# A triangular inverse in a RWKV stage: its 128x128 transposes become 64x64 products with an identity

## The reference, cut to what matters

```
def step(S, inp):
    wt, kkt, kat, kt, vt, rt = inp
    S = (S * wt[..., None, :]
         - jnp.einsum('...vk,...k->...v', S, kkt)[..., :, None] * kat[..., None, :]
         + vt[..., :, None] * kt[..., None, :])
    return S, jnp.einsum('...vk,...k->...v', S, rt)
```

## Time and profile before

| | |
|---|---|
| median of 3 runs | 1917.11 us (1916.86 to 1919.38) |
| profiled execution, its span (the time that its profile gives) | 1921.7 us |
| PE busy | 1734.6 us, 90% of the span |
| granted TensorE clock, mean | 0.948 of full speed |
| RWKV stage, both directions with what lies between | about 606 to 864 us |

### The profile page before, as it was taken

One profiled execution on the slowest core, in us unless ns is written; L12 is line 12 of the kernel. 1 busy time (PEld: TensorE's weight loads), 2 busy tenths in 40 slices (PEclk: granted clock), 3 DMA queues, 4 the chain that ended last, 5 costly groups with the idle time before them and its releaser, 6 DMA issues.

```text
span 1921.7 us, 32920 instructions
## 1 busy us (share of the span) xinstructions
PE 1734.6 (90%) x14129; PEld 1449.6 (75%) x14129; DVE 736.9 (38%) x1219; ACT 639.3 (33%) x1208; POOL 550.2 (29%) x498
## 2 busy tenths in 40 slices
PE   7997899799876983989999787999999999999998
PEld 5886778688655762768997686888888888888886
DVE  3105888233175547554232425120332133113307
ACT  4214887323255432433243424221211112111122
POOL 4213753221044315315234010222222222222221
PEclk9998999899878995998999997999999999999999
DMA  5110000121000000002312010111111111111112
GB/s 183 50 59 1 1 1 1 31 69 34 17 1 6 4 3 0 5 3 98 128 59 85 17 47 20 49 46 49 50 50 45 55 49 41 48 56 49 45 44 93
DMA packets 61200, 81.27 MB, mean 42 GB/s; under 512 B 4610, under 2 KB 49824, under 8 KB 61056
## 3 DMA queue, kind: packets, MB, share of 16 engines
q1 hardware_dynamic: 60112, 76.60, 12.9%
q0 software_dynamic: 944, 2.58, 0.6%
HBM read 74.96 MB, written 4.19 MB: 41 GB/s over the span
## 4 chain that ended last, share of the span: by engine, by line
PE 79%; DVE 11%; ACT 5%; issue 2%; DMA 1%; POOL 1%; SPq 0%; DVEq 0%; ACTq 0%
PE PS L1511 13%; PE PS L1512 13%; PE PS L1514 13%; PE PS L1764 7%; PE PS L2064 4%; PE PS L2062 4%; PE PS L2063 4%; PE PS L1524 4%; PE PS L1525 3%; PE PS L1526 3%; PE PS L1622 3%; PE PS L1656 2%; PE PS L1828 2%; PE PS L1648 1%; DVE E__70 L1083 1%
## 5 line engine op out<-in xcount | busy, mean ns | idle before, releaser
L421 POOL TENSOR_TENSOR WL<-RAW,WH 128x512 fp32r<-128x512 f32 x226 | 308.6, 1375 | 945.5 <-ACT WH L581 945.4
L1511 PE MATMUL PS<-HH,WH 128*128 128x512 f32 x1072 | 420.7, 392 | 10.9 <-POOL WL L421 8.0
L1512 PE MATMUL PS<-HL,WH 128*128 128x512 f32 x1072 | 419.6, 391 | 0.0
L581 ACT ACTIVATE WH<-RAW 128x512 fp32r<-128x512 f32 x226 | 140.2, 631 | 642.9 <-PE PS L1514 310.2
L1514 PE MATMUL PS<-HH,WL 128*128 128x512 f32 x1072 | 331.5, 391 | 0.0
L1511 PEld LDWEIGHTS PS<-HH,WH 128*128 128x128 f32 x1072 | 202.7, 189 | 53.9 <-issue 8.3
L1514 PEld LDWEIGHTS PS<-HH,WL 128*128 128x128 f32 x1072 | 202.5, 189 | 42.4
L1512 PEld LDWEIGHTS PS<-HL,WH 128*128 128x128 f32 x1072 | 202.9, 189 | 41.9
L1461 DVE TENSOR_TENSOR FU<-PS,ACTB 128x512 f32<-128x512 f32 x44 | 27.3, 684 | 469.1 <-PE PS L1514 469.1
L2062 PE MATMUL PS<-WH,AH 128*128 128x512 f32 x352 | 136.9, 389 | 0.0
L2063 PE MATMUL PS<-WL,AH 128*128 128x512 f32 x352 | 136.9, 389 | 0.0
(11 more groups left out here) (296 smaller groups left out, 2817.0 us busy)
## 6 DMA issues: line engine op xcount, KB each, us to landing
RAW<-in_ffn_w_gu SPq DMA_DIRECT2D x88, 256.0 KB, 2.8
RAW<-in_w_in SPq DMA_DIRECT2D x48, 256.0 KB, 2.8
RAW<-in_ffn_w_down SPq DMA_DIRECT2D x44, 256.0 KB, 2.6
XT<-in_x SPq DMA_DIRECT2D x8, 512.0 KB, 5.1
RAW<-in_w_out SPq DMA_DIRECT2D x16, 256.0 KB, 2.7
X<-in_x SPq DMA_DIRECT2D x8, 512.0 KB, 8.3
RAW<-in_x_wkv SPq DMA_DIRECT2D x16, 256.0 KB, 2.7
out_x<-FO SPq DMA_DIRECT2D x8, 512.0 KB, 2.6
```

The lines of the kernel that those rows point to most:

```text
L421: pool.tensor_tensor(w_low, RAW[:, p % NRAW], w_high.bitcast(F32), ALU.subtract).then_inc(w_lo, 1)
L581: act.activation(split_at(p)[0], RAW[:, p % NRAW], ACT.Copy).then_inc(w_hi, 1)
L1511: pe.matmul(where(ct, i), wh[:, k, c], ah(kt)[:, t0:t0 + n], start=first and starts(ct, i), stop=False, skip_group_check=True)
L1512: pe.matmul(where(ct, i), wh[:, k, c], al(kt)[:, t0:t0 + n], start=False, stop=False, skip_group_check=True)
```

## The change

Each turn of Q is made by eight 64x64 products, Q's block as the stationary operand and a 64x64 identity as the moving one, in the order of `blocks()`, in place of two 128x128 transposes. The output of block (ct, hp, c) now goes to bank c at column 64 ct. So the two readers take it from there, and the copies stay as they are.

```diff
 def inverse_t(j):
-    for ct in range(2):
-        mm = pe.transpose(PS[:, (j.slot.a, j.slot.b)[ct], 256:384], j.slot.Q[:, 2 * ct:2 * ct + 2, :].rearrange("p h k -> p (h k)"), ID)
+    for ct, hp, c, rh, rc in blocks():
+        mm = mm1(PS[rh, (j.slot.a, j.slot.b)[c], 256 + 64 * ct:320 + 64 * ct], j.slot.Q[rc, 2 * ct + hp, :], I64[rc])
     return mm
...
 def inverse(j, l):
...
-        mm = mm1(PS[rc, (sl.a, sl.b)[hp], 64 * ct:64 * ct + 64], sl.XQ[rh, ct, 3, c, :], sl.XQ[rh, c, 2, ct, :])
+        mm = mm1(PS[rc, (sl.a, sl.b)[hp], 64 * ct:64 * ct + 64], sl.XQ[rh, c, 3, ct, :], sl.XQ[rh, c, 2, ct, :])
...
 def wu(j):
...
-        mm = mm1(PS[rc, (sl.a, sl.b)[hp], P * ct:P * ct + P], sl.XQ[rh, ct, 3, c, :], sl.XQ[rh, c, 0:2, ct, :])
+        mm = mm1(PS[rc, (sl.a, sl.b)[hp], P * ct:P * ct + P], sl.XQ[rh, c, 3, ct, :], sl.XQ[rh, c, 0:2, ct, :])
```

## The result

The changed kernel takes 1937.63 us (median of 4 runs, 1933.82 to 1943.67), the kernel before in the same comparison 1918.24 us (1916.86 to 1922.29). The ratio is 1.0097, with an interval of 1.0071 to 1.0123: about 19 us slower, where 12 us faster was forecast.

A forecast was written before the change was run, and what follows sets the result against it. PE, 90% busy, with a nearly full queue and a DVE tail, bounds the steady period. Savings of 3.7 + 0.3 + 0.7 + 0.4 + 0.55 + 0.1 = 5.75 us a direction, 11.5 for both, give 1917.1 - 11.5 = 1905.6 us; range 1899 to 1913.

The forecast's parts named there:

- the walk: Step-by-step timing of the stage through engine queues and waits, with a turn at 0.235 us: 5.75 us saved a direction.
- Rival 1: At each turn: only two quarters overlap, so the products cost 0.47 us; 1915 us in all; chance 0.12.
- Rival 2: In the steady periods: more PE idle time lowers the clock to 1.2 GHz, slower, from 1921.6 us; chance 0.05.
- Rival 3: In each fill: products instead of transposes raise the clock earlier, 5 us more gain, 1900.6 us; chance 0.12.
- one steady period: From one job's turn to the same turn of the next: 11.50 us becomes 10.76, five such a direction, 3.7 us.
- the chain from 611.12 to 630.93: First periods of the stage, a chain of single steps: said to hold six turns, with gains of 0.3 and 0.7 us.
- The fill's terms: Gains while the stage fills, a direction: 0.3 us first period, 0.7 for the next three turns, 0.4 third period.

The follow-up runs named there:

- experiment 1: Kernel before with 28 or 14 empty instructions ahead of each turn, or 224 ahead of each feed-forward step: ratios 0.9997, 1.0002, 1.0010.

## Why the prediction was wrong

**What it got right.** A turn on quarters holds PE for 0.24 us, as taken from the nearest row, and the cost ahead of it is gone. The floor of 25 ns from start to start, which the prediction cites from the Trainium skill (TensorE: Matmul & The Clock Gate, "Wait — 56ns, not 53.3ns?"), is contradicted once more: 16 records in 0.24 us. Where no issue wait falls the walk holds roughly: with one turn changed, steady periods of 11.35 us where it gave 0.18 less than 11.49, and a first period (from the first key transposes to the second) of 8.55 us in the changed kernel, where the kernel before took 8.83 in another execution (its program ran again in experiment 1) and the walk gave 0.3 less. In the second period it gave too much: 0.7, where 9.07 to 9.16 became 8.80.

**The rivals.** Rival 1 is out: the turn takes 0.24 us. Rival 2, the falling clock, came in small: two stretches at 0.5 in the second direction's steady part, 6.8 us together. It isn't the cause, since the first direction had 1.00 in all its steady periods and was late all the same, by 6.6 us. The prediction had argued against it from 701 to 705 us, where PE was busy 1.86 of 4 us at 1.00; in the same trace the clock fell to 0.5 at 705.7 and stayed there to 712.5. Rival 3 isn't seen: the first period has a second stretch at 0.5 in two executions of the kernel before (10.65 us) and none in two others (8.83), so this goes by the execution.

**The step that failed** is the sum of "one steady period": the walk had PE, DVE, ACT and POOL in it, but not the supply of PE's program. It came to 10.76 us with 938 instructions (so many the trace has from one steady period to the next), 3.7 blocks of 256, so 2.9 us a block. Nothing in it asked whether a block can be had in 2.9 us. The pace while PE was short of instructions was 3.69 us a block (numbers 7617 to 10689, 634.49 to 678.80, in the changed kernel). That gives 938 / 256 x 3.69 = 13.5 us; 13.5 and 13.1 were measured. The first of these holds the stretch from which the pace was read and is no test of it; the second, and the other kernels in the table above, are. The kernel before, with 770, needs 11.1 us by the same pace and ran at 11.49: it was 0.4 us from this bound, and its cheap turns of four instructions in 0.57 us were what kept it off. The prediction came near it once. It noted 15 ns for a record, 7.5 ns for an instruction, as a proof that 16 small products are cheap. That is the rate within a burst; over a stretch it was 14.4 ns an instruction (3.69 us / 256), and eight products take 0.24 us of PE's time and 32 x 14.4 = 0.46 us of the supply's.

**The sum again.** 28 more instructions a turn, 96 turns, are 2688, 10.5 blocks, and 11 more packets were counted. At 3.69 us that is 38.7 us. Measured were 19. The rest went into the slack of the kernel before: 0.4 us a period in the steady part, and in the fill and drain, where PE waits for others and blocks last 4 us and more. Stage by stage, from the first to the last key transposes of a direction the changed kernel took 83.3 and 86.7 us, the kernel before 76.7 and 77.6: 15.8 of the 19 us; the last two periods of each direction hold the remainder.

**How sure this is.** Shown: the waits lie at one place of a block of 256, in seven kernels; they shrink when work with few instructions is added (26.0 to 10.0 us); the loss shrinks when instructions are taken from elsewhere (19.4 to 10.8 us); half of the change costs nothing that can be told from none. Not shown: a loss made by adding instructions and nothing else, since both ways that I tried failed: the empty instructions never ran, and the increments had a price of their own. Nor is it shown what sets the 1.40 us from a packet's landing to PE's next instruction. The Trainium skill (Runtime: NRT & Kernel Launch, "Instruction fetch mechanics") says that each engine's program is streamed in blocks of 16 KiB, 256 instructions, by the sequencer's own queue; the packets and the place of the waits agree. It also calls the cost mostly hidden. In this stage it isn't: 26 us.

Two statements ahead need mending. `results` has 80 matmul records a job (40 calls, two each), not 144; the walk took its duration from rows, so no number hangs on it. And the chain from 611.12 to 630.93 has nine turns, not six: two in the first period, four in the second, three in the third. The fill's terms were worked out for six; since all of them together are 1.4 us a direction, this doesn't change the outcome.

## What to carry to other kernels

Count the instructions of a stretch as well as its work. Here TensorE was not fed faster, over a stretch, than 256 instructions in some 3.5 to 3.7 us. A single block can go faster when the one ahead of it was slow: the kernel before has blocks of 2.9 us, each behind one of 4.7 to 4.8, and no ten in a row averaged under 3.49 in any kernel here with transposes or products as turns. So a stream of fp32 products on quarters (four instructions each) runs out of program long before it runs out of array. A change that trades a few long instructions for many short ones pays only where the stretch uses its blocks slowly. To look for this in a profile: waits put down to "issue" in the middle of a group, and a growing packet count of the instruction queue.

A loss of the size that a theory gave is not that theory's proof. Two other forms of the turn lost the same 20 us without one issue wait, by work alone.

## What the runs showed of the hardware that I had not expected

- PE resumed after a shortage 1.4 us (median) after a 16 KB packet of its instruction queue had landed. The median block in the stage lasted 3.7 us in the changed kernel and 4.1 in the kernel before.
- A turn as a full-width fp32 product holds PE 0.64 us, as four products of 64 rows by 128 columns 0.59, as two transposes 0.37, and as eight quarter products 0.24.
- Semaphore increments on PE's queue start 0.151 us apart; 2688 of them added 417 us.
- Empty instructions put into PE's program never reached the chip: the packet count stayed at 112.
- With PE short of instructions, the granted clock fell to 0.5 twice, 6.8 us together, inside steady periods of the second direction; from 785 to 850 us the kernel before kept 1.00.
